# Fourteen seven-product units a layer for thirteen, one at the end of each feed-forward part

## What is computed

```python
def conv_ffn(h, p):
    u = h @ p['w_up']
    t = u.shape[1]
    pad = CONV_WIDTH // 2
    up = jnp.pad(u, ((0, 0), (pad, pad), (0, 0)))
    w = p['conv_w']
    u = up[:, 0:t] * w[0] + up[:, 1:t + 1] * w[1] + up[:, 2:t + 2] * w[2] + p['conv_b']
    a, gt = u[..., :D_FF], u[..., D_FF:]
    return (a * jax.nn.silu(gt)) @ p['w_down']
```

## Time and profile before

| | |
|---|---|
| median of 3 executions | 2469.86 us (2467.2 to 2470.62) |
| the profiled execution | 2468.28 us, its span 2466.5 us |
| granted TensorE clock, mean | 0.997 |
| busy: PE, PEld, DVE, ACT, POOL | 97%, 88%, 63%, 43%, 19% |
| matmuls | 16631 records |
| read from HBM | 196.51 MB, 81 GB/s over the span |

### The profile page before, as it was taken

How to read it: one execution, slowest core, us unless ns; L and a number is a source line. 1 busy time by engine, 2 the same in 40 slices (tenths; PEclk the granted TensorE clock), 3 DMA queues, 4 the chain that set the end, 5 groups by cost and what they waited for, 6 DMA issues and landing times.

```text
span 2466.5 us, 41961 instructions
## 1 busy us (share of the span) xinstructions
PE 2396.8 (97%) x16631; PEld 2178.5 (88%) x16631; DVE 1560.3 (63%) x2834; ACT 1061.6 (43%) x1952; POOL 472.9 (19%) x412
## 2 busy tenths in 40 slices
PE   8999999999999999999999999999999999999999
PEld 6878977798799999999977799778977999999999
DVE  4675366636755875847657743775476569568483
ACT  5454255424533542524444533553245255345252
POOL 0500022033010222404004001220310104033130
PEclk9999999999999999999999999999999999999999
DMA  8212232322133122333232022331210422232222
GB/s 270 82 35 69 76 114 94 126 79 61 25 97 103 53 85 72 83 86 86 92 105 77 18 78 67 99 102 61 82 52 19 137 69 69 69 99 65 77 81 83
DMA packets 254660, 203.32 MB, mean 82 GB/s; under 512 B 10384, under 2 KB 237698, under 8 KB 254466
## 3 DMA queue, kind: packets, MB, share of 16 engines
q1 hardware_dynamic: 247362, 197.68, 26.5%
q10 hardware_dynamic: 7104, 2.95, 0.4%
HBM read 196.51 MB, written 4.10 MB: 81 GB/s over the span
## 4 chain that ended last, share of the span: by engine, by line
PE 91%; DVE 4%; ACT 3%; issue 2%; POOL 0%; DMA 0%; SPq 0%; ACTq 0%; DVEq 0%; POOLq 0%
PE ps L1856 22%; PE ps L1742 16%; PE ps L1880 12%; PE ps L1764 8%; PE ps L1967 6%; PE ps L1981 4%; PE ps L1727 3%; PE ps L1729 3%; PE ps L1728 3%; PE ps L2015 3%; PE ps L1906 1%; PE ps L1599 1%; ACT prob L2269 1%; PE ps L2005 1%; PE ps L1813 1%
## 5 line engine op out<-in xcount | busy, mean ns | idle before, releaser
L2805 DVE TENSOR_TENSOR wlo<-raw,whi 128x512 fp32r<-128x512 f32 (+1 forms) x238 | 184.7, 780 | 180.5 <-ACT whi L2335 180.5
L2335 ACT ACTIVATE whi<-raw 128x512 fp32r<-128x512 f32 (+1 forms) x238 | 145.9, 615 | 311.4 <-PE ps L1856 241.2
L2552 DVE TENSOR_TENSOR wlo<-raw,whi 128x1024 fp32r<-128x1024 f32 (+2 forms) x136 | 168.9, 1243 | 173.3 <-ACT whi L2136 172.3
L2913 POOL TENSOR_TENSOR rstd<-smean,mhalf 128x4 f32<-128x4 f32 (+3 forms) x96 | 114.1, 1192 | 518.2 <-DVE smean L2613 517.4
L2136 ACT ACTIVATE whi<-raw 128x1024 fp32r<-128x1024 f32 (+2 forms) x136 | 139.2, 1024 | 167.5 <-PE ps L1742 105.1
L2641 DVE TENSOR_REDUCE negmax<-ps 128x1 f32<-128x640 f32 x192 | 150.9, 819 | 61.7 <-PE ps L1967 60.7
L2269 ACT ACTIVATE prob<-ps,negmax 128x640 f32<-128x640 f32 x192 | 150.5, 791 | 68.1 <-DVE negmax L2641 68.1
L1764 PE MATMUL ps<-hhi,whi 128*128 128x320 f32 x512 | 176.3, 344 | 1.5 <-issue 1.5
L1856 PE MATMUL ps<-ahi,whi 128*128 128x320 f32 x698 | 159.1, 309 | 0.0
L1856 PE MATMUL ps<-alo,whi 128*128 128x320 f32 x698 | 159.1, 309 | 0.0
L1856 PE MATMUL ps<-ahi,wlo 128*128 128x320 f32 x698 | 159.0, 309 | 0.0
(11 more groups left out here) (321 smaller groups left out, 6573.4 us busy)
## 6 DMA issues: line engine op xcount, KB each, us to landing
raw<-in_w_up SPq DMA_DIRECT2D x88, 512.0 KB, 5.1
raw<-in_w_in SPq DMA_DIRECT2D x40, 1024.0 KB, 5.3
raw<-in_w_ada SPq DMA_DIRECT2D x29, 1024.0 KB, 5.4
raw<-in_w_down SPq DMA_DIRECT2D x32, 512.0 KB, 3.7
adaw<-in_w_ada SPq DMA_DIRECT2D x8, 1024.0 KB, 12.5
raw<-in_w_o SPq DMA_DIRECT2D x8, 1024.0 KB, 5.0
raw<-in_w_down SPq DMA_DIRECT2D x16, 384.0 KB, 3.2
raw<-in_w_branch_a SPq DMA_DIRECT2D x4, 1024.0 KB, 6.7
```

What stands on the lines that cost most here:

```text
L2552: dve.tensor_tensor(dst(wlo), src, dst(whi).bitcast(F32), ALU.subtract).then_inc(S["lo_ready"], 1)
L2805: dve.tensor_tensor(ring_of(wlo, s["ring"], w), block_source(s), ring_of(whi, s["ring"], w).bitcast(F32), ALU.subtract)\
```

## The change

One line: which up units of each part are made with seven products.

```diff
-SEVEN = [(4, 5, 6), (0, 1, 2, 4, 5, 6), (0, 1, 2, 4)]
+SEVEN = [(4,5,7),(0,1,2,4,5,7),(0,1,2,4,5)]
```

## The result

| | before | after |
|---|---|---|
| median of 13 executions each, on one chip | 2468.86 us (2466.23 to 2470.62) | 2475.4 us (2474.31 to 2477.22) |
| the profiled execution, its span | 2468.28, 2466.5 | 2474.61, 2472.8 |
| granted TensorE clock, mean | 0.997 | 0.996 |
| matmul records | 16631 | 16607 |

The ratio is 1.0028 with an interval of 1.002 to 1.0035: the change makes the kernel about 6.5 us slower. The forecast was +3.2.

The account below looks back on a forecast made before the run. It took the feed-forward to be bound by TensorE's count of matmuls plus its few waits. -3.52 - 1.46 + 7.2 + 1.0 = +3.2 us gave 2473 us, own range 2469.5 to 2476.5, 8-in-10 range 2466 to 2480.

Parts of the forecast that it names:

- Point 1: Feed-forward products: one more seven-product unit a layer saves 2 x 12 matmuls at 0.1467 us, 3.52 us less on PE.
- Point 2: Waits within runs of seven-product up units fall from 3.50 to 2.04 us: 1.46 us less, bounds 0.8 and 2.5.
- Point 3: At part ends, down tile 1 waits for the last up unit's G taps: 0.68 us four times, 1.56 us twice.
- the template: Earlier trace where seven-product unit 6 precedes an ordinary unit; its read-out times, G taps ending at T0+3.99, served the forecast.
- T0: The moment at which PE may start the first down product of a part.
- Point 4: At part ends, down tile 1's later load makes the wait 0.8 us four times, 2.0 us twice: 7.2 us more.
- rows 5: Cited trace rows of the read-out sequence behind seven-product unit 6; their 1.10 us DVE split gave the upper bound 9.2.
- Point 5: Last tile's activation low half at part ends: hidden in parts 0 and 1, 0.5 us twice in part 2, 1.0 more.
- Covered: PE does not wait at down tile 1 and at the last tile: -5.0, so 2464.9 us; chance 0.07.
- The load lands still later: The six part-end down loads take 1.2 us more than assumed: 7.2 more, +10.4, so 2480.3 us; chance 0.15.
- PE's clock falls after a wait: Part 2's wait of 2.0 us brings 3.5 us at half speed, 1.75 us twice: +6.7, so 2476.6 us; chance 0.13.

Follow-up runs that it names:

- the early load: Changed kernel, but down unit 1's weights load right behind unit 0's, into the free half of unit 0's slot: 2465.86 us, ratio 0.9993.
- part 2's end alone: Kernel before, with only part 2 getting its extra seven-product unit at its end: 2471.23 us, ratio 1.0013.
- again: The kernel listed just before it, unchanged, run once more for one profile: changed kernel 2476.36 us, extra unit in part 2 only 2472.03 us.
- runs of two plain: Kernel before with its 13 seven-product units a layer in runs of at most two, loads and PSUM pairs unedited: 2470.49 us, ratio 1.0006.
- the kernel with pair 1: Changed kernel, but down unit 1 accumulates in free PSUM pair 1 instead of pair 3, its load still late: 2471.22 us, ratio 1.0011.

## Why the prediction was right in its time and wrong in its terms

The time, 2475.4, is 2.4 above the forecast of 2473 and inside the range. That it is so near is in part luck. The ends cost 6.8 us more than forecast and the runs gave 1.7 more, in opposite directions; and the median of before is 1.0 us lower in this comparison than the 2469.86 that the forecast stands on. As a difference, +6.5 was measured for +3.2. It lies behind the 2474.8 at which the prediction begins to call the kernel slower, a case to which it gave 0.32 against 0.63 for a time within 0.2%.

**Point 1, products:** right; 24 records fewer, and the pace is 0.1467 us a matmul in every kernel.

**Point 2, runs:** the direction was right, the size was half. The step that failed is "Unit 5 becomes the last of its run, and I give it the 0.34 us that the last ones show". The row measured the third of a run of three, not the last of a run. In after the last of each run of two waits 0.05 to 0.06 us, six of six, while the runs (0, 1, 2), which the change leaves alone, kept their waits: 3.56 us before, 3.54 after. In the two kernels without a run of three no seven-product unit waits over 0.06. So the gain was 3.50 - 6 x 0.05 = 3.2, outside the bound of 2.5. That bound was itself mis-sized: with the 0.04 us that it names as its condition, four ends of runs give 2.7 and all six 3.3. What ties the 0.34 to the third unit was not tested; the view of waits names DVE's mixes in front of it.

**Point 3, the read-out:** right, as the early load showed: 0.57 to 0.65 for the 0.68 of the template. For part 2 it worked out 1.56 at tile 1; 1.2 was measured. The last mix ends where the template has it, at T0+0.2; the split behind it, of 384 columns instead of 512, begins 0.1 us earlier and is shorter (0.91 us for 1.10), so that the G taps end at T0+3.68 instead of +3.99.

**Point 4, the late load:** the wait was rightly named, its price was not. What the prediction foresaw is there. SP's queue and ACT in order of time, the late loads and the waiting splits of both ends:

```profile
898.46 0.37 SPq L1515 DMA_DIRECT2D raw<-in_w_down  x1
...
902.60 1.15 ACT L2335 ACTIVATE whi<-raw 128x512 fp32r<-128x512 f32 x2 [3.13 <-DMA raw<-in_w_down]
903.66 0.72 ACT L2367 ACTIVATE ahi<-va 128x640 fp32r<-128x640 f32 x1
...
1195.77 0.37 SPq L1515 DMA_DIRECT2D raw<-in_w_down  x1
...
1199.17 0.94 ACT L2335 ACTIVATE whi<-raw 128x384 fp32r<-128x384 f32 x2 [4.08 <-DMA raw<-in_w_down]
```

The issues stand at T0-5.39 and T0-3.87, to the hundredth where the prediction put them, and ACT's split starts 4.14 and 3.40 us behind them, for 3.7 and 3.2 from the earlier trace rows: 0.2 to 0.4 us of the error. ACT's waits for `raw` on its DMA sum to 20.1 us, six of them, where before has none. The rest is in what follows on DVE and POOL, here at part 0's end and, last two lines, at part 2's:

```profile
903.26 0.69 DVE L2805 TENSOR_TENSOR wlo<-raw,whi 128x512 fp32r<-128x512 f32 x1 [3.07 <-ACT whi L2335]
...
904.52 1.87 POOL L2956 TENSOR_TENSOR alo<-va,ahi 128x640 fp32r<-128x640 f32 x1 [11.85 <-ACT ahi L2367]
904.87 0.49 DVE L2833 TENSOR_TENSOR ps<-wu,ps 128x320 f32<-128x320 f32 x1
905.27 1.67 DVE L2805 TENSOR_TENSOR wlo<-raw,whi 128x512 fp32r<-128x512 f32 x1
906.87 2.04 DVE L2845 SCALAR_TENSOR_TENSOR vg<-ps,PT,vg 128x127 f32<-128x127 f32 x4
...
1200.81 1.78 POOL L2956 TENSOR_TENSOR alo<-va,ahi 128x640 fp32r<-128x640 f32 x1 [12.14 <-ACT ahi L2367]
1201.47 1.54 DVE L2805 TENSOR_TENSOR wlo<-raw,whi 128x384 fp32r<-128x384 f32 x1
```

ACT's rounding of the unit before (`ahi`) stands behind its waiting split, as the prediction says; it sets off POOL's subtraction for that unit's `alo` at 904.52, and this now runs to 906.39, just over DVE's last split. That split takes 1.67 us instead of 0.69 and ends at 906.94, 0.55 behind POOL's end. The G taps end at T0+5.06, where the prediction has 4.1. With a split of 0.69 they would end at T0+4.08: the step of point 4 that failed is the length of this last split, about 1 us at each end. In part 2 it takes 1.54 instead of 0.55, and the taps end at T0+5.33 for 4.45. The prediction did name POOL's stretching, at "the 1.10 us of rows 5", but as its upper bound only, though the 3.99 of point 3 already holds it. POOL's row beside that split, before the change and in the early load, shows where it comes from:

```profile
891.67 1.57 POOL L2956 TENSOR_TENSOR alo<-va,ahi 128x640 fp32r<-128x640 f32 x1 [11.86 <-ACT ahi L2367]
...
903.73 1.57 POOL L2964 TENSOR_TENSOR alo<-va,ahi 128x640 fp32r<-128x640 f32 x1 [10.91 <-DVE wlo L2813]
904.75 1.10 DVE L2813 TENSOR_TENSOR wlo<-raw,whi 128x512 fp32r<-128x512 f32 x1 [0.23 <-ACT whi L2343]
```

In the template POOL ends at 893.24 and the split at 893.79, in the early load at 905.30 and 905.85: 0.55 us each time, as in after. It is so at every part end with a seven-product last unit in every profile: the split of 512 columns ends 0.54 to 0.55 us behind POOL's subtraction, that of 384 columns 0.41 to 0.42, wherever between T0-0.3 and T0+1.7 the subtraction starts. So it is POOL's end that sets the G taps. In after POOL starts 0.8 us later than in the early load, behind ACT's waiting split and `ahi`, and takes 0.3 us longer: together the 1.07 us by which part 0's end is dearer.

By the Trainium skill, page "SBUF — State Buffer", section "Who interferes with whom", a VectorE instruction with two SBUF inputs and a GpSimd instruction that reads SBUF contend for their shared ports, which the section calls an exclusive lock. The traces agree with it: 0.55 us is less than the 0.69 that a whole split takes, so within 0.14 us the split ran as if from POOL's end on, and the same holds for 0.41 against 0.55. No run took POOL's subtraction away with the load left late, so this share is read from the rows, not shown by an experiment; that the late load with all that hangs on it costs 0.9 to 1.1 us an end in parts 0 and 1 and 1.6 in part 2 is shown by the early load.

**Point 5, the low half:** right. Hidden in parts 0 and 1 (its end is T0+10.1, a microsecond later than forecast, and so is PE), 0.4 us in part 2 where the clock stays up, for 0.5. Only its last sentence did not come: with the early load the wait is 0.4 us too, not longer, since both PE's first wait and the tile's own chain start from the end of the G taps.

**The rivals.** "Covered" is out: PE waits at all six ends. "The load lands still later" with 1.2 us more is out as such, 0.4 and 0.2 were the most measured. "PE's clock falls after a wait" had a chance of 0.13 and came true in both layers of after and of its repetition; a falling clock behind these waits was also one of the prediction's own signs of being wrong. Its argument against itself, that PE is full on both sides of the wait, does not hold. Its price of 1.75 us was too high: an end with a fall in after costs 4.4, of which 2.8 are the wait, so 1.6 went in the fall, and 0.5 us of restart and wait for `alo`, which part 2's end alone shows, vanished behind it: 1.1 net.

The ends thus measured 15.0 for 8.2: 5.8 for the read-out with the low half, where the terms of points 3 and 5 make 6.8; 7.1 for the late load (15.0 less the 5.8 of the early load less the clock), where point 4 added 1.4; and 2.1 for the clock, which the sum had at nothing. That the runs gave 1.7 more hid a part of it.

## What to carry to other kernels

When a reordering puts a load behind a later step, count who queues behind the engine that waits for it, including work of a third engine that is thereby moved onto a busy one: here a late load that was forecast to cost 0.1 to 0.5 us an end beyond the read-out cost 0.9 to 1.6. A free half of a buffer that lets the load go early was worth 8.7 us by the medians where the reordering itself lost 6.5. And a wait that is read at the end of a run belongs to its position and length: look at a run of the length that you will have before you give it a price.

## What the runs showed of the hardware that I had not expected

The clock fell behind some waits and not behind others of the same length. Waits of PE at a part end, with full work on both sides:

| wait of PE | falls of the clock |
|---|---|
| up to 1.8 us | none |
| 2.7 to 2.8 us | 5 of 10 (after 2 of 2, again 2 of 2, end 2 alone 0 of 2, again 1 of 2, runs of two plain 0 of 2) |
| 3.2 to 3.3 us | 2 of 2 |

In after PE went at the slower pace for 3.3 us behind one wait and 3.6 behind the other, in layer 1 of the kernel with pair 1 for about 5.5. The table holds for waits with full work around them: in the earlier trace rows the clock fell behind a wait of 1.78 us, where PE had been short of work before. The same kernel had it in one layer and not in the other, so what decides is not in the program alone; what it is stays open. For a forecast this means a chance and a price, here 1.1 us net for each fall of the shorter kind.

The late loads of 512 KB landed 3.9 to 4.1 us behind their issue and those of 384 KB 3.4, where the medians of before are 3.7 and 3.2; ACT's split started 0.02 us behind each landing. So what was later than forecast is the landing itself, not a step behind it. In after the medians over all down loads are 3.9 and 3.5, so these six are not slower than the others beside them.
